# Rows of an expert spread over 128 partitions, and three full transposes in place of eight narrow ones

## What is computed

```
h        = rmsnorm(x, moe_norm)                  # 512 x 1024
group    = argmax(h @ router_group)              # 1 of 4
top 2 of 8 experts of that group, with gates     # 32 experts in all
y_expert = (silu(h @ w1[e]) * (h @ w3[e])) @ w2[e]   # w1, w3: 1024 x 512, w2: 512 x 1024
x        = x + sum of the two gates * y_expert
```

## Time and profile before

| | us |
|---|---|
| median of 3 runs | 1946.04 |
| lowest, highest | 1940.31, 1950.17 |
| span of the profiled execution, first to last instruction | 1948.6 |
| TensorE busy in it | 1610.3 (83%) |
| VectorE, ScalarE, GpSimd busy | 645.1, 432.4, 196.4 |
| mean rate of all DMA | 253 GB/s |

### The profile page before, as it was taken

One profiled execution on the slowest core, in us unless ns is written; L12 is line 12 of the kernel. 1 busy time (PEld: TensorE's weight loads), 2 busy tenths in 40 slices (PEclk: granted clock), 3 DMA queues, 4 the chain that ended last, 5 costly groups with the idle time before them and its releaser, 6 DMA issues. The chain is left out here.

```text
span 1948.6 us, 25751 instructions
## 1 busy us (share of the span) xinstructions
PE 1610.3 (83%) x10464; PEld 868.9 (45%) x10593; DVE 645.1 (33%) x1106; ACT 432.4 (22%) x790; POOL 196.4 (10%) x234
## 2 busy tenths in 40 slices
PE   7999898879699788887784999789699887888783
PEld 5756587644433333332331779555433332333231
DVE  5557867682311111101113532872311111110113
ACT  5253343371101000000002411761110000000001
POOL 2002534310100000000002000540100000000001
PEclk9999899899799998888987899999799898988896
DMA  6431000119589999999995220208699999999994
GB/s 168 136 113 34 6 4 3 34 56 369 209 339 399 400 400 401 401 396 391 391 374 189 80 93 1 87 4 367 215 375 397 404 397 401 398 393 387 384 356 151
DMA packets 106262, 492.30 MB, mean 253 GB/s; under 512 B 31392, under 2 KB 62112, under 8 KB 81056
## 3 DMA queue, kind: packets, MB, share of 16 engines
q1 hardware_dynamic: 93344, 461.26, 61.9%
q0 software_dynamic: 4608, 16.78, 2.2%
q10 hardware_dynamic: 8192, 12.59, 1.9%
HBM read 461.24 MB, written 29.36 MB: 252 GB/s over the span
## 5 line engine op out<-in xcount | busy, mean ns | idle before, releaser
L671 PE MATMUL ps<-w_unit,xT 128*48 128x512 f32 x1024 | 519.3, 666 | 153.8 <-DMA w_unit<-in_moe_w 151.2
L672 PE MATMUL ps<-w_unit,xT 128*48 128x512 f32 x1024 | 520.2, 667 | 0.0
L671 PEld LDWEIGHTS ps<-w_unit,xT 128*48 128x48 f32 x1024 | 135.6, 137 | 509.9 <-issue 506.8
L710 DVE TENSOR_TENSOR xT<-ps,gain 128x384 f32<-128x384 f32 x64 | 35.7, 557 | 748.6 <-PE ps L661 748.6
L700 PE MATMUL ps<-w_unit,hidT 128*48 128x512 f32 x512 | 235.5, 603 | 4.0 <-ACT hidT L727 3.1
L701 PE MATMUL ps<-w_unit,hidT 128*48 128x512 f32 x512 | 235.6, 603 | 0.0
L727 ACT ACTIVATE hidT<-ps 128x192 f32<-128x192 f32 x64 | 21.2, 331 | 657.6 <-PE ps L692 655.2
L1124 PE MATMUL ps<-hT_high,w_high 128*128 128x512 f32 (+1 forms) x344 | 141.2, 410 | 7.2 <-PE ps L1126 3.7
L1126 PE MATMUL ps<-hT_high,w_low 128*128 128x512 f32 (+1 forms) x344 | 137.5, 400 | 0.0
L1125 PE MATMUL ps<-hT_low,w_high 128*128 128x512 f32 (+1 forms) x344 | 137.4, 400 | 0.0
L672 PEld LDWEIGHTS ps<-w_unit,xT 128*48 128x48 f32 x1024 | 135.4, 137 | 0.0
(11 more groups left out here) (361 smaller groups left out, 2140.9 us busy)
## 6 DMA issues: line engine op xcount, KB each, us to landing
w_unit<-in_moe_w SPq DMA_DIRECT2D x188, 2048.0 KB, 38.5
x_rows<-sorted_rows SPq DMA_DIRECT2D x64, 192.0 KB, 43.1
expert_rows<-y ACTq DMA_DIRECT2D x128, 96.0 KB, 7.8
w_raw<-in_od_w_qkv SPq DMA_DIRECT2D x12, 1024.0 KB, 5.2
w_raw<-in_ev_w_in SPq DMA_DIRECT2D x10, 1024.0 KB, 6.3
w_unit<-in_moe_w SPq DMA_DIRECT2D x8, 1024.0 KB, 36.2
sorted_rows<-bias SPq DMA_DIRECT2D x32, 192.0 KB, 5.7
w_unit<-in_ev_w_out SPq DMA_DIRECT2D x2, 2048.0 KB, 10.8
```

Of the source, the lines that this page charges most:

```text
L671: nc.tensor.matmul(ps_1[b][0:MB, :], xT[b][:, k, :], w1[:, k, :], start=k == 0, stop=k == KD - 1)
L672: last = nc.tensor.matmul(ps_3[b][UP:UP + MB, :], xT[b][:, k, :], w3[:, k, :], start=k == 0, stop=k == KD - 1)
```

## The change

Three things belong together.

1. ScalarE writes `xn` with its columns grouped by chunk: column k*128+p of the new tile is feature p*8+k. It reads `x` in steps of 8 elements for that. The scatter moves whole rows of 4 KB as before.
2. `load_rows` reads the same 48 rows, 192 KB, as 384 pieces of 512 B (one chunk of one row) and puts them on all 128 partitions: row i*16+r, chunk k goes to partition r*8+k, place i. `x_rows` is 128 x 3 x 128 now.
3. `turn_rows` makes three transposes of 128x128, and `gain_rows` reads the bank in steps of 8 elements, since a column of it is now row*8+chunk.

```diff
-                nc.scalar.activation(xn[:, t, :], x[:, t, :], ACT.Copy, scale=rstd[:, t:t + 1]).then_inc(xn_done, 1)
+                nc.scalar.activation(xn[:, t, :].rearrange("p (k q) -> p k q", k=KD),
+                                     x[:, t, :].rearrange("p (q k) -> p k q", k=KD), ACT.Copy,
+                                     scale=rstd[:, t:t + 1]).then_inc(xn_done, 1)
...
+XG = MB * D // (P * P)
...
-    x_rows = [c.sb(f"x_rows{j}", [MB, D], ctx=ctx) for j in range(SLOTS)]
+    x_rows = [c.sb(f"x_rows{j}", [P, XG, P], ctx=ctx) for j in range(SLOTS)]
...
     def turn_rows(pe, j, u):
         pe.wait_ge(rows_in[j], 16 * u + 16)
         nc.tensor.ldweights(c.half[:, :], tile_position=(0, 0))
-        for k in range(KD):
-            last = nc.tensor.transpose(ps_x[:, k * MB:(k + 1) * MB], x_rows[j][:, k::KD], c.ident[0:MB, 0:MB])
+        for i in range(XG):
+            last = nc.tensor.transpose(ps_x[:, i * P:(i + 1) * P], x_rows[j][:, i, :], c.ident[:, :])
         last.then_inc(xT_done, 1)
...
-        nc.vector.tensor_tensor(xT[b][:, :, :], ps_x[:, 0:KD * MB].rearrange("p (k m) -> p k m", m=MB),
+        nc.vector.tensor_tensor(xT[b][:, :, :], ps_x[:, 0:KD * MB].rearrange("p (m k) -> p k m", k=KD),
...
     def load_rows(sp, j, row):
-        sp.dma_start(x_rows[j][:, :], xrows[bass.ds(row, MB), :]).then_inc(rows_in[j], 16)
+        rows = xrows[bass.ds(row, MB), :].rearrange("(i r) (k n) -> (r k) i n", i=XG, k=KD)
+        sp.dma_start(x_rows[j][:, :, :], rows).then_inc(rows_in[j], 16)
```

## The result

The changed kernel takes 1874.76 us (median of 4 runs, 1872.44 to 1877.87) against 1944.76 for the kernel before (4 runs). The ratio of the two is 0.964, 95% interval 0.9611 to 0.9669. The profiled execution has a span of 1870.7 us, 77.9 us less than 1948.6. Medians and ratios here leave out an execution over 1.5% above the fastest of its kernel; only the run with 64 partitions, 0 to 63, had such, two of ten.

A forecast was written before the change was run, and what follows sets the result against it. The DMA transfer queue was taken as the bound. 54 row loads x 1.10 us = 59.4, plus 3.5 at the start, gave 62.9 us less than the 1948.6 span, 1885.7; adjusted to the runs' median, 1883 us, range 1872 to 1909.

The forecast's parts named there:

- DMA is the bound, TensorE and VectorE are not: Experts' stages: the transfer queue sets the end; TensorE could do 12.25 us per expert, against 16.14 predicted after the change.
- The stall of 1.10 us per load: Weight stream while a row load lands: rate falls to 308 GB/s for 4 us; spreading rows over 128 partitions removes it.
- Its cause: Row loads: 48 partitions take bytes more slowly than 16 DMA engines bring them, and weights bound for these partitions wait too.
- Small pieces: Row loads in 384 pieces of 512 B instead of 48: 0.21 to 0.43 us added per load, 0.21 taken.
- The drift: DMA engines drifting apart in the experts' stages: 17.24 us pace against 16.84 mean; half of 0.40 us per load counted gone.
- The thin end of a layer: Sign at a layer's end: whether the 6 us of thin DMA, share down to 0.38, remain settles whether engines still drift apart.
- The start: Before down(0) in each layer: three shorter transpose turns save 1.8 us, 3.5 us for both layers; ends 0 and 3.5.
- ScalarE at nothing: L417 reading `x` in steps of 8: 0 to double its 1.15 us, hidden by 6.7 us of cover, so no cost.
- Rival A: Row loads: only the load's own slow rate goes, 0.5 us per load, 1915 us in all; chance 0.11.
- B: Row loads: small pieces mixed with weight packets cost all that the spread gives, 1943 us; chance 0.05.
- C: Row loads: the stall stays whatever the partitions, say because of the source, and pieces add cost, 1960 us; chance 0.08.
- the wait for weights: Sign at TensorE before L671: waiting falls from 151 us by some 28, as each of 54 experts arrives 1.10 us sooner.

## Why the prediction was right, and where it was off

The forecast was 1883 us, 62.9 less; measured were 70.0 less between the medians. By its steps:

- *DMA is the bound, TensorE and VectorE are not.* Right. The share stays 1.01, and eight transposes for three cost 3.2 us in all.
- *The stall of 1.10 us per load goes.* Right: 415 GB/s around a landing for 308, and 0.47 us by the totals, 0.63 by the pace, left of the load's price.
- *Its cause.* Half right. "The 48 partitions are what differs" held, as the two runs with 64 partitions show. "Few partitions take the bytes more slowly" did not: 64 that are every second one lose nothing, and 120 evenly filled ones lose 0.6 us per load. "Weights bound for these partitions wait too" is borne out so far that the weights' packets beside the rows took 743 ns for 618. Which weights wait, and at what, stays open; that the row load must be dealt out over the engines as the stream is fits the runs if the transfer to every second partition is dealt out so too, and is not shown. The Trainium skill's port rule ("SBUF — State Buffer", "Door 1: The DMA port swizzle"), which I quoted, counts the ports that a transfer reaches, and would have let 120 partitions through.
- *Small pieces, 0.21 us, of 0.21 to 0.43.* 0.15 to 0.16 measured: 15.88 against 15.73 computed, and 15.72 with one piece. That lies between the 0.09 and the 0.21 that the prediction worked out. In a full stream they are cheaper than the relative taken from the router.
- *The drift, half of 0.40.* This is the mis-sized term. Nearly all of it went: with one piece the pace is 15.72, what the bytes take at 425 GB/s, and by the prediction's own measure 0.08 is left in the changed kernel, 15.88 less the 15.80 that 6.685 MB take at 423 GB/s. It went with the stall, so I take the two to have one cause, which is argued. The thin end of a layer, which was to settle it, got shorter and remains. At 54 loads the other half is 10.8 us, the small pieces' 0.06 is 3.2, and together they are more than the 7 us by which the forecast was short; the stretch right behind expert 5's load, where the pace was not yet steady, gave less than 1.36 us per load (69.6 us in place of 73.4).
- *The start, 3.5 us.* 3.4 measured between stage start and expert 5's load. That is luck in part: the run with eight transposes ascribes 2.4 of it to them, and the rest has another source.
- *ScalarE at nothing.* The duration came near its upper bound, 2.15 us for 1.15, and the cover held: `xn` is ready at 507.3 us, 5.7 before the last tile's scatter at 512.98.
- *Rival A* (the load's own rate alone) left 1.06 us per load and falls with 0.63 at most; *B* falls with 15.88 us, *C* with the run on every second partition.

One sign that I had named was wrong in size: the wait for weights fell from 151.2 to 134.3 us, 17 and not 28. TensorE needed less by more than the prediction counted: the transposes took 35.0 us for 69.0, and the pairs of matmuls in `up`, which run side by side, 499.3 for 519.3. These 54 us, taken from the 70 by which the weights came sooner, leave 16; no run tests this.

## What to carry to other kernels

In a stage that streams weights at a full DMA share, look for windows with the share at 1 and the rate down, and name the transfer that lands in them; its price here was four times its bytes, 1.92 us for 0.46. Give such a transfer the partition shape of the stream, 128 partitions, before thinking of its pieces, and then make each partition's piece as long as the layout allows: the first was worth 70 us here, the second some 9 more by the pace and 12.8 measured. Turning such data costs next to nothing while TensorE waits for the same stream: five more transposes for each expert cost 3.2 us.

## What the runs showed of the hardware beyond that

- ScalarE reading float32 in steps of eight elements took 2.15 us for 1.15 (128x1024); VectorE reading a PSUM bank in the same steps took 558 ns for 557 (128x384).
- TensorE loading 128x128 float32 as weights took 142 ns from adjacent columns (the changed kernel's transposes) and 188 from every eighth one (L363).
- SP stood 3.8 to 4.4 us in the issue of a row load of 384 pieces in the full stream, 0.43 as a rule with 48; the landing came 33.0 us after the issue for 43.1 (medians). At 423 and 397 GB/s that is 14 MB issued ahead for 17 MB, so the queue held fewer bytes when some came in small pieces. No cost is seen: only later loads of the same full queue stood behind it.
